# One layer with four token mixers on one core: branch A's recurrence two blocks of 128 tokens at a time

## What is computed

```python
sa = einsum('bhvk,bhk->bhv', S, -kk_t)
S = (S * w_t[:, :, None, :] + sa[..., None] * (kk_t * a_t)[:, :, None, :]
     + v_t[..., None] * k_t[:, :, None, :])
y_t = einsum('bhvk,bhk->bhv', S, r_t)
```

## Time and profile before

| | |
|---|---|
| median of three runs | 1105.72 us (1105.67 to 1106.65) |
| profiled execution, first to last instruction | 1106.6 us |
| PE busy | 1075.6 us, 97% |
| DVE, POOL, ACT busy | 595.6, 375.6, 319.9 us |

### The profile page before, as it was taken

How to read it: one execution, slowest core, us unless ns; L and a number is a source line. 1 busy time by engine, 2 the same in 40 slices (tenths; PEclk the granted TensorE clock), 3 DMA queues, 4 the chain that set the end, 5 groups by cost and what they waited for, 6 DMA issues and landing times.

```text
span 1106.6 us, 23043 instructions
## 1 busy us (share of the span) xinstructions
PE 1075.6 (97%) x9992; PEld 830.4 (75%) x9992; DVE 595.6 (54%) x1068; ACT 319.9 (29%) x533; POOL 375.6 (34%) x343
## 2 busy tenths in 40 slices
PE   7999999999999999999999999999999999999997
PEld 5686787767677777777777786877878777887885
DVE  3768933986555332343443118647778587423543
ACT  4545113321521221221221033144545341001221
POOL 1431533312356312212212233244434239762000
PEclk9999999999999999999999999999999999999999
DMA  9700111200100101101111021120101126412221
GB/s 352 259 20 9 48 50 47 76 29 24 40 26 26 49 25 35 40 25 36 37 29 31 28 68 33 44 58 26 50 25 37 39 68 242 143 39 95 95 76 58
DMA packets 80133, 70.28 MB, mean 64 GB/s; under 512 B 4128, under 2 KB 68896, under 8 KB 80032
## 3 DMA queue, kind: packets, MB, share of 16 engines
q1 hardware_dynamic: 74560, 49.34, 14.3%
q10 hardware_dynamic: 5472, 19.47, 4.8%
HBM read 64.60 MB, written 4.19 MB: 62 GB/s over the span
## 4 chain that ended last, share of the span: by engine, by line
PE 88%; DVE 7%; POOL 2%; DMA 1%; ACT 1%; issue 1%; SPq 1%; DVEq 0%; ACTq 0%; POOLq 0%
PE bank L591 53%; PE bank L1104 8%; PE bank L640 8%; PE bank L692 2%; PE bank L1059 1%; DVE slots L1678 1%; PE bank L919 1%; PE bank L915 1%; DMA slots<-in_w_mod 1%; PE bank L797 1%; PE bank L861 1%; PE bank L884 1%; DVE slots L1662 1%; PE bank L972 1%; POOL y_lo L477 1%
## 5 line engine op out<-in xcount | busy, mean ns | idle before, releaser
L591 PE MATMUL bank<-hn_hi,w_hi 128*128 128x512 f32 x880 | 363.0, 412 | 5.8 <-ACT slots L1216 2.3
L591 PE MATMUL bank<-hn_lo,w_hi 128*128 128x512 f32 x880 | 344.4, 391 | 0.0
L591 PE MATMUL bank<-hn_hi,w_lo 128*128 128x512 f32 x880 | 343.8, 391 | 0.0
L506 POOL CAST w_hi<-w_raw 128x512 fp32r<-128x512 f32 x110 | 87.0, 791 | 556.6 <-PE bank L591 556.6
L591 PEld LDWEIGHTS bank<-hn_hi,w_hi 128*128 128x128 f32 x880 | 165.3, 188 | 47.7 <-issue 6.9
L591 PEld LDWEIGHTS bank<-hn_hi,w_lo 128*128 128x128 f32 x880 | 165.6, 188 | 36.4
L591 PEld LDWEIGHTS bank<-hn_lo,w_hi 128*128 128x128 f32 x880 | 165.8, 188 | 32.0 <-issue 1.9
L508 POOL TENSOR_TENSOR w_lo<-w_raw,w_hi 128x512 fp32r<-128x512 f32 x110 | 156.2, 1420 | 8.8
L1238 ACT ACTIVATE stage<-bank 128x512 f32<-128x512 f32 x64 | 37.2, 598 | 160.8 <-PE bank L591 141.9
L1216 ACT ACTIVATE slots<-bank 128x512 f32<-128x512 f32 x42 | 24.6, 598 | 123.0 <-PE bank L591 123.0
L1837 DVE TENSOR_TENSOR stage<-stage,bank 128x512 f32<-128x512 f32 x48 | 33.0, 687 | 49.8 <-PE bank L640 48.6
(11 more groups left out here) (329 smaller groups left out, 1604.9 us busy)
## 6 DMA issues: line engine op xcount, KB each, us to landing
w_raw<-in_w_in SPq DMA_DIRECT2D x110, 256.0 KB, 2.8
slots<-in_w_mod SPq DMA_DIRECT2D x16, 512.0 KB, 11.4
slots<-in_x SPq DMA_DIRECT2D x8, 512.0 KB, 9.6
w_branch<-in_w_branch SPq DMA_DIRECT2D x32, 128.0 KB, 2.6
slots<-in_w_mod ACTq DMA_DIRECT2D x8, 512.0 KB, 5.4
slots<-in_w_out ACTq DMA_DIRECT2D x8, 512.0 KB, 6.3
xr<-in_x ACTq DMA_DIRECT2D x8, 512.0 KB, 3.5
out<-xr ACTq DMA_DIRECT2D x8, 512.0 KB, 2.6
```

The costliest lines, as they stand in the source:

```text
L506: nc.gpsimd.tensor_copy(w_hi[p][:, :, :], w_raw[p][:, :, :]).then_inc(s_pool_step, 1)
L591: last = mm(o, w[p][:, k4, :], h[:, k, n * HALF:(n + 1) * HALF], start=(p == 0 and k4 == 0 and q == 0), stop=(p == 1 and k4 == 3 and q == 2))
```

## The change

Blocks are taken in pairs s (four of them), b = 0, 1 within a pair. The operands are decayed in place over two blocks of a slot (`prep_queries`, `prep_keys`); b and k are no longer multiplied by the end decay, which DVE applies to G after each state update instead (`e_end`). The product rk moves from behind the stage into `prep_queries`. The diagonal blocks come out of M by mask and sum instead of by their own matmuls. All small groups up to U serve both blocks, and P, U and W lie in slots 14, 15 and 10, 11. The calls of fill are redistributed; the reciprocals stand one behind each level of the first pair and one at the start of its chunks k = 0, 1, 2. Merge halves are placed anew in DVE's and ACT's order. In the diff below PE's loops come first, then ACT's, then DVE's.

```diff
-            def rwkv_products(i):
-                ts = slice(i * P, (i + 1) * P)
-                if i:
-                    pe.wait_ge(s_a_y_ready, 2 * i)
-                    pe.wait_ge(s_a_g_ready, 4 * i)
-                pe.wait_ge(s_a_ends_ready, i + 1)
-                turn(bank[4][:, 0:128], slot(12)[:, ts])
-                turn(bank[4][:, 128:256], slot(13)[:, ts])
...
+            def rwkv_products(s):
+                if s:
+                    pe.wait_ge(s_a_y_ready, 4 * s)
+                    pe.wait_ge(s_a_g_ready, 4 * s)
+                pe.wait_ge(s_a_ends_ready, s + 1)
+                for b in range(2):
+                    ts = slice((2 * s + b) * P, (2 * s + b + 1) * P)
+                    for q, src in enumerate((12, 13, 4, 5)):
+                        last = turn(bank[4 + 2 * b][:, q * P:(q + 1) * P], slot(src)[:, ts])
+                    last.then_inc(s_a_tm1_done, 1)
+                    for q, src in enumerate((14, 15, 10, 11)):
+                        last = turn(bank[5 + 2 * b][:, q * P:(q + 1) * P], slot(src)[:, ts])
+                    last.then_inc(s_a_tm2_done, 1)
+                fill(3)
+                pe.wait_ge(s_a_tm_ready, 4 * s + 4)
+                for b in range(2):
+                    for a, src in enumerate((14, 10)):
+                        for j in range(2):
+                            for c in range(2):
+                                t64 = slice((2 * s + b) * P + c * C, (2 * s + b) * P + (c + 1) * C)
+                                for par in range(2):
+                                    r = slice(64 * par, 64 * par + 64)
+                                    last = mm(bank[4 + 2 * b + par][64 * c:64 * c + 64,
+                                                                    (2 * a + j) * P:(2 * a + j + 1) * P],
+                                              slot(src + j)[r, t64], slots[r, j:j + 5:4, t64], start=True, stop=True)
+                    last.then_inc(s_a_m_done, 1)
+                fill(4)
+
...
-                fill(2 if i else 1)
-                pe.wait_ge(s_a_tm_ready, 2 * i + 2)
...
-                last.then_inc(s_a_a_done, 2)
-                fill(1)
...
-            def rwkv_inverse(i):
+            def rwkv_inverse(s):
                 for l in range(1, 5):
-                    pe.wait_ge(s_a_x_ready, 6 * i + l)
-                    blocks32(lambda h, q, b, o, at: mm(bank[5][q, o], m13(h)[q, b], Td[q, h, :], start=True, stop=True,
-                                                       tile_position=at)).then_inc(s_a_v_done, 1)
+                    pe.wait_ge(s_a_x_ready, 6 * s + l)
+                    blocks32(lambda b, h, n, q, cols, o, at: mm(
+                        bank[5][q, o], m_of(b, 0, h)[q, cols], Td[q, n, :], start=True, stop=True,
+                        tile_position=at)).then_inc(s_a_v_done, 1)
                     fill(1)
-                    pe.wait_ge(s_a_v_ready, 5 * i + l)
-                    blocks32(lambda h, q, b, o, at: mm(bank[6][q, o], v_lev[q, h, :], Ud[q, h, :], start=True, stop=True,
-                                                       tile_position=at)).then_inc(s_a_dx_done, 1)
-                    fill(1)
...
+                    pe.wait_ge(s_a_v_ready, 5 * s + l)
+                    blocks32(lambda b, h, n, q, cols, o, at: mm(
+                        bank[6][q, o], v_lev[q, n, :], Ud[q, n, :], start=True, stop=True,
+                        tile_position=at)).then_inc(s_a_dx_done, 1)
+                    fill(2)
+                pe.wait_ge(s_a_x_ready, 6 * s + 5)
+                for b in range(2):
...
                 last.then_inc(s_a_dx_done, 1)
-                each(lambda h, r, c: mm(bank[4][r, h * C:(h + 1) * C], m24(h)[r, 0:C], tm1[r, h * C:(h + 1) * C], start=True, stop=True)).then_inc(s_a_p_done, 1)
-                pe.wait_ge(s_a_x_ready, 6 * i + 6)
-                pe.wait_ge(s_a_uu_ready, 2 * i + 2)
-                each(lambda h, r, c: mm(bank[6 + c][64 * (h % 2):64 * (h % 2) + 64, (h // 2) * C:(h // 2 + 1) * C], tm1[r, 256 + h * C:256 + (h + 1) * C], UU[r, h, :], start=True, stop=True)).then_inc(s_a_w_done, 1)
+                each(lambda b, h, r, c: mm(bank[4][r, 256 * b + h * C:256 * b + (h + 1) * C], m_of(b, 1, h)[r, C:2 * C],
+                                           tm1[b][r, h * C:(h + 1) * C], start=True, stop=True)).then_inc(s_a_p_done, 1)
+                fill(2)
+                pe.wait_ge(s_a_x_ready, 6 * s + 6)
+                pe.wait_ge(s_a_uu_ready, 2 * s + 2)
+                each(lambda b, h, r, c: mm(
+                    bank[6 + c][64 * (h % 2):64 * (h % 2) + 64, b * P + (h // 2) * C:b * P + (h // 2 + 1) * C],
+                    tm1[b][r, 256 + h * C:256 + (h + 1) * C], UU[r, nth(b, h), :], start=True, stop=True))\
+                    .then_inc(s_a_w_done, 1)
                 fill(1)
-                pe.wait_ge(s_a_p_ready, i + 1)
-                each(lambda h, r, c: mm(bank[5][r, h * C:(h + 1) * C], UU[r, h, :], p_sb[r, h * C:(h + 1) * C], start=True, stop=True)).then_inc(s_a_u_done, 1)
-
...
-                fill(1)
+                fill(1 if n == 15 else 2)
                 pe.wait_ge(s_a_sa_ready, 2 * n + 2)
...
                 last.then_inc(s_a_gnew_done, 1)
-                fill(1 if c == 0 else 4 if i + 1 < NT else 1)
-
-            for i in range(NT):
-                rwkv_products(i)
-                rwkv_inverse(i)
-                rwkv_chunk(i, 0)
-                rwkv_chunk(i, 1)
+                if n < 15:
+                    fill(3 if n % 4 == 3 else 2)
+
+            for s in range(NT // 2):
+                rwkv_products(s)
+                rwkv_inverse(s)
+                for b in range(2):
+                    for c in range(2):
+                        rwkv_chunk(s, b, c)
             project(4)
             pe.wait_ge(s_a_y_ready, 16)
-            pe.wait_ge(s_a_g_ready, 32)
+            pe.wait_ge(s_a_g_ready, 16)
...
+            def decays(s):
+
+                ends = two_blocks(0, s).rearrange("p j (n t) -> p n j t", t=C)[:, :, :, C - 1]
+                if s == 0:
+                    act.wait_ge(s_a_g_zero, 1)
+                else:
+                    act.wait_ge(s_a_u_done, s)
+                if s >= 2:
+                    act.wait_ge(s_a_g_ready, 4 * (s - 1))
+                nc.scalar.activation(e_end[:, s % 2], ends, ACT.Exp).then_inc(s_a_e_ready, 1)
                 after(s_a_e_ready)
-                if i:
-                    act.wait_ge(s_a_ends_ready, i)
-                nc.scalar.activation(Em.rearrange("p (j c) t -> p j c t", c=2), b4, ACT.Exp, scale=-1.0)\
-                    .then_inc(s_a_e_ready, 1)
+                nc.scalar.activation(Em, two_blocks(0, s), ACT.Exp, scale=-1.0).then_inc(s_a_e_ready, 1)
+                after(s_a_e_ready)
+                act.wait_ge(s_a_e_ready, 3 * s + 2)
+                nc.scalar.activation(two_blocks(0, s), two_blocks(0, s), ACT.Exp).then_inc(s_a_e_ready, 1)
                 after(s_a_e_ready)
...
                 merge_gate()
-                if i + 1 < NT:
-                    decays(i + 1)
-                act.wait_ge(s_a_x_ready, 6 * i + 5)
...
-                merge_gate()
+                    if k == 0:
+                        merge_gate()
+                        if s + 1 < NT // 2:
+                            decays(s + 1)
+                    elif k == 2:
+                        merge_gate()
...
+            def prep_queries(s):
+
+                e64 = two_blocks(0, s).rearrange("p j (n t) -> p j n t", t=C)
+                kk64 = two_blocks(4, s).rearrange("p j (n t) -> p j n t", t=C)
+                dve.wait_ge(s_a_e_ready, 3 * s + 3)
+                nc.vector.tensor_tensor(kk64[:, :, :, 1:C], kk64[:, :, :, 1:C], e64[:, :, :, 0:C - 1], MUL)\
+                    .then_inc(s_vector_step, 1)
+                after(s_vector_step)
+                nc.vector.tensor_tensor(two_blocks(14, s), two_blocks(14, s), Em, MUL)
+                dve.wait_ge(s_vector_step, counts[s_vector_step.name])
+                nc.vector.tensor_tensor(two_blocks(0, s), two_blocks(8, s), two_blocks(0, s), MUL)\
+                    .then_inc(s_vector_step, 1)
+                dve.wait_ge(s_vector_step, after(s_vector_step))
+                cols = slice(2 * P * s, 2 * P * (s + 1))
+                for j in range(2):
+                    nc.vector.scalar_tensor_tensor(out=slot(8 + j)[:, cols], in0=slot(8 + j)[:, cols],
+                                                   scalar=pc("rk", j), in1=slot(10 + j)[:, cols], op0=MUL,
+                                                   op1=MUL).then_inc(s_a_rk_ready, 1)
+                    after(s_a_rk_ready)
+
+            def prep_keys(s):
+
+                dve.wait_ge(s_a_rk_ready, 2 * s + 2)
+                nc.vector.tensor_tensor(two_blocks(10, s), two_blocks(10, s), Em, MUL).then_inc(s_a_ends_ready, 1)
                 dve.wait_ge(s_a_ends_ready, after(s_a_ends_ready))
...
+            def ret_norm(z):
+
```

(90 more changed lines are left out.)

258 lines of the change are left out of this document (98 added, 160 removed).

## The result

The changed kernel takes **1097.38 us** (median of four runs, 1097.14 to 1098.49), the kernel before 1105.70 (four runs, 1104.83 to 1106.65): a ratio of 0.9917, 95% interval 0.9901 to 0.9933, or 8.3 us saved. Forecast were 11.9 saved and 1093.8 us, in a range of 1085 to 1102. Another five runs of it, beside the experiments, gave 1097.24 us and a ratio of 0.9913 (0.9896 to 0.9930).

A forecast was written before the change was run, and what follows sets the result against it. PE's own matmul stream was taken as the bound. Small groups -17.0, stage end -3.0, and a stall with its clock loss +8.1 gave -11.9 us off the 1105.7 median: 1093.8 us, range 1085 to 1102 (own range 1088 to 1098).

The forecast's parts named there:

- What bounds it: Branch A's recurrence: PE's own matmul stream is the bound, busy 329.67 of 332.60 us, with 156 pieces before and after.
- Toll and level groups: PE's small groups: each costs a 0.21 us toll; nine pairings save 0.29 us each, 2.61 per two blocks.
- Products: Transposes, M and diagonal products on PE: 5.20 us per two blocks before, 4.32 after, 0.88 saved.
- The last dU, P and W: PE's groups ending each pair: 3.62 us per two blocks before, 2.85 after, 0.77 saved.
- All groups: PE's small groups over the four pairs: 4.26 us saved per pair, 17.0 in all, bounds 14.2 and 20.6.
- End of the stage: At project(4): a shorter gap behind the last merge and no clock fall save 3.0 us, bounds 1.3 and 3.6.
- POOL's lateness: First half of tile 4: PE stalls 6.4 us, once, for w_lo, which POOL delivers late behind the eighth reciprocal.
- Clock behind the stall: After PE's wait for w_lo: reduced clock charged at 1.7 us, as behind an earlier gap of 1.96 us.
- Cover (1): After the M products: DVE's 5.3 us diagonal chain is covered by fill(4), 5.5 us, and a toll; costed at nothing.
- The prediction's own sign of being wrong: In the recurrence: PE waiting for DVE in every pair, on issue behind the level groups, or nowhere would refute it.
- rival C: Diagonal chain outruns fill(4) by 1 us in four pairs, clock falling each time: 10.8 us more, 1104.6; chance 0.08.
- Rival D: Doubled 64-record level groups run PE's instruction queue dry, 36 x 0.9 = 32 us, giving 1126 us; chance 0.07.

The follow-up runs named there:

- the groups taken apart: Changed kernel with the second group of levels 1 to 4 (16 groups of 64 records) split again into two blocks of 32 records: 1101.65 us, ratio 0.9954.
- the early reciprocals: Changed kernel with its eight retention-norm reciprocals moved, three ahead of the first pair's masks, one behind each of five levels: 1090.76 us, ratio 0.9856.
- the end undone: Changed kernel with the last merge and the last branch piece put back behind the last state update and products: 1100.97 us, ratio 0.9946.
- the last experiment: Changed kernel with the reciprocals moved early and the second pair's prep_queries moved to the third chunk, diagonal products still read from SBUF: 1088.75 us, ratio 0.9835.

## Why the prediction was right, and where not

- **What bounds it**: right. PE's stream, with the same pieces, and its waits explain the difference.
- **Toll and level groups**: right, and shown by the groups taken apart. The 256 records less came; but the stage's small groups have 3776 records and had 4032, not 3840 and 4096: I had counted two records for each of the 64 transposes, and in the trace a transpose is one. 2.5 us per pair against 2.61.
- **Products**: saved 1.32 per pair, not 0.88. The 16 transposes last 1.66 us to the next large matmul, not 1.94, the M products 1.91, not 2.06: I doubled 0.97 and 1.03 with their start-up in them. The last dU, P and W gave 0.86, not 0.77. All groups: 18.9 instead of 17.0.
- **End of the stage**: -2.9 in the two traces, as 3.0 was forecast, but 1.6 of it is clock that the median execution of before seems not to have lost. (The stretch of half clock lasted 3.4 us; half the clock costs half of it.) Of 29 executions of it beside the experiments, 14 took 1105.0 to 1106.8 us and 15 took 1107.3 to 1108.6, with a lower mean clock (mostly 0.996 against 0.998); the shown median belongs to the first kind, the profile, with its stretch of half clock at project(4), by its total (about 1108.4, see below) to the second. That this stretch is what makes the second kind is not shown: two more waits of 1.7 us stand in that kernel, for ACT ahead of the stage and for POOL's w_lo at 927 us, and in the profiles of other kernels such a wait was followed by a stretch like it (from 277.5 and 277.9 us, and from 907 and 922).
- **POOL's lateness**: right in place, cause and size, 6.03 against 6.4. The prep took 2.8 us instead of 3.1, which is most of the difference.
- **Clock behind the stall**: 1.7 charged; 4.0 lost in the profiled execution, 1.5 in the next one. I had one row for a thing that varies.
- **Cover (1)**: the step that failed. "Thin: if this cover is gone it is that much per pair", and it was costed at nothing. The prediction's own sign of being wrong came true in this: PE waits for DVE in every pair. From the next large matmul behind the M products (293.87) to the transpose's end (300.23) the chain took 6.4 us, not 5.3: the products took 2.62 where I had 1.64, the first sum 0.92 where I had 0.41, beside POOL's passes, which is what rival C named; it cost 0.70 us four times, **2.8 us**. I had priced every operation by its shortest row, though the earlier trace rows had a like one at five times that. Rival C's clock falls didn't come: gaps of 0.7 us left the clock at full speed.
- **Rival D**: no wait on issue in the stage; branch B's are as before.

In the two profiled executions the terms come to -18.9 - 2.9 + 6.0 + 4.0 + 2.8 = -9.0 us, and the spans differ by 11.6. The other 2.6 us are in none of these terms, and I can't assign them: 0.5 before the stage and 1.5 in branch B and behind it, where PE's instructions are the same, and 0.6 within the stage. Against the median -8.3 is to be met: without the 1.6 of clock at the stage's end, -18.9 - 1.3 + 6.0 + 2.8 give -11.4; with 1.3 to 4.1 of clock behind the stall that is -10.1 to -7.3. My statement that the profiled span stands at the longest run (1106.6 and 1106.65) was the wrong base, too: in all 29 executions the total is about 1.8 us over the span, so that the profiled one was a run of about 1108.4.

That 1097.38 lies within my own range (1088 to 1098), near its upper end, is partly luck: 2.8 us of waits that I had at nothing and 1.7 of clock that the median of before seems not to have lost stand against 1.9 us more from the groups and 0.4 less stall, and the rest is a clock price that I had from one row.

## What to carry to other kernels

Work that one engine does late for another, once, inside a long fixed order, is found by counting the pieces that its consumer has left; the sum of the small savings is not safe until every such order (here POOL's) is followed to its end. A cover that is thin by the shortest durations of its chain is no cover where another engine's two-operand passes run beside it: price the chain by the slow rows, too. When a stall is taken away, look at what it had kept apart; here the early reciprocals gave back 2 us until prep_queries moved as well. And before a difference of a few us is put down to one gap of PE, look through the whole trace for half clock: in two profiles here 1.6 us of it lay in a part that no edit touched.

## What the hardware showed unexpectedly

**Half clock behind a gap is a draw.** Behind the same gap of PE (6.01 to 6.03 us in six profiled executions) the stretch at the 1.2 GHz level differed from execution to execution: PE ran on at 0.43 us per large matmul for 2.7 to 9 us, at a price of 1.3 to 4.1 us. Behind the gaps of 0.70 us the matmuls stayed at full clock. Behind the wait of 1.7 us for ACT ahead of the stage, which every kernel here has, the clock fell in two of the twelve profiles, and behind the wait of 1.7 to 1.9 us for w_lo at 904 to 927 us in two others. Behind the gap at project(4) it fell in both profiles with a long one (1.96 us, the kernel before; 2.61, the end undone). The wait of 2.1 us at the third chunk, in two profiles, was followed by no fall before the next gap. One of the falls behind w_lo, in the kernel of the last experiment (PE; a large matmul takes 0.63 us at half clock, 0.39 at full):

```profile
906.17 0.47 PE L590 MATMUL bank<-hn_hi,w_hi 128*128 128x512 f32 x1 [1.85 <-POOL w_lo L507]
...
907.71 0.63 PE L590 MATMUL bank<-hn_hi,w_lo 128*128 128x512 f32 x1
```

**DVE and POOL lock each other out, but not beside every pass.** A DVE product with two SBUF operands took 2.87 us beside a POOL pass of 2.70, and 0.69 with POOL idle. That is the rule of the Trainium skill, "SBUF — State Buffer", section "SBUF: two separate sides": a DVE operation with two SBUF inputs and a POOL operation that reads SBUF exclude each other for a whole instruction. The traces agree with it in the places shown above, beside POOL's passes with two operands and beside its casts. Beside its pass with one tensor operand (L535) they do so only in part. In the changed kernel:

```profile
354.47 0.96 DVE L1989 TENSOR_TENSOR stage<-stage,tab 128x128 f32<-128x128 f32 x1
355.46 0.69 DVE L1897 TENSOR_TENSOR slots<-slots,tab 128x512 f32<-128x512 f32 x1
...
354.17 2.85 POOL L535 TENSOR_SCALAR slots<-slots,par 128x1024 f32<-128x1024 f32 x1
```

L1989 is held (0.29 us elsewhere). But the product of prep_keys, also with two SBUF operands, takes no longer inside the same pass than with POOL idle (0.69 us), and the pass is no longer for it: it took 2.85 us, too, in the kernel with the reciprocals early, where DVE had no such operation beside it. Why the two differ no run here shows.
